# Two-layer hybrid decoder trunk on one core: eight split weight groups in flight at the passage from cross-attention to the up-projection, one token tile first

## What is computed

```python
for l in range(DEPTH):
    y = hybrid_mixer(rms_norm(h, mix_norm_pre[l]), ...)          # attention + convolution heads, one projection out
    h = h + rms_norm(y, mix_norm_post[l])
    y = memory_cross_attention(rms_norm(h, x_norm_pre[l]), rms_norm(mem, mem_norm[l]), wq, wk, wv, wo)
    h = h + rms_norm(y, x_norm_post[l])
    y = conv_ffn(rms_norm(h, ffn_norm_pre[l]), w_up, conv_w, conv_b, w_down)
    h = h + rms_norm(y, ffn_norm_post[l])

def memory_cross_attention(h, mem_n, wq, wk, wv, wo):            # 4 heads of 256, 256 memory tokens
    ...
    return softmax(q k / 16) v @ wo

def conv_ffn(h, w_up, conv_w, conv_b, w_down):                   # w_up: 1024 x 5632, w_down: 2816 x 1024
    u = causal_depthwise_conv(h @ w_up, conv_w, conv_b)          # width 3
    gate, val = u[..., :D_FF], u[..., D_FF:]
    return (gelu(gate) * val) @ w_down
```

## Time and profile before

| | |
|---|---|
| median of 3 runs | 868.9 us (868.72 to 869.17) |
| the profiled execution, its own time | 868.48 us |
| its span, first to last instruction | 866.5 us |
| TensorE busy | 832.1 us (96%) |
| VectorE busy | 616.6 us (71%) |
| ScalarE busy | 498.8 us (58%) |
| mean granted TensorE clock | 0.991 of full speed |

### The profile page before, as it was taken

How to read it: one execution, slowest core, us unless ns; L and a number is a source line. 1 busy time by engine, 2 the same in 40 slices (tenths; PEclk the granted TensorE clock), 3 DMA queues, 4 the chain that set the end, 5 groups by cost and what they waited for, 6 DMA issues and landing times.

```text
span 866.5 us, 13183 instructions
## 1 busy us (share of the span) xinstructions
PE 832.1 (96%) x5252; PEld 742.7 (86%) x5252; DVE 616.6 (71%) x1081; ACT 498.8 (58%) x761; POOL 28.4 (3%) x53
## 2 busy tenths in 40 slices
PE   3999999999979999999999999999998999999997
PEld 2898898888859999988899889887986899999885
DVE  5689986664467877886576999757546587777643
ACT  4655876555447666564454578655645566665441
POOL 1000000010010000000010000001001000000000
PEclk9999999999989999999999999999998999999999
DMA  9555344472344565556646553447433555655651
GB/s 343 206 175 184 105 146 142 150 253 88 121 146 171 196 194 175 178 183 219 193 152 238 168 167 112 139 139 240 149 99 100 166 178 188 196 191 176 206 181 48
DMA packets 40364, 147.33 MB, mean 170 GB/s; under 512 B 4528, under 2 KB 4656, under 8 KB 40304
## 3 DMA queue, kind: packets, MB, share of 16 engines
q1 hardware_dynamic: 38144, 138.90, 49.4%
q0 software_dynamic: 2160, 7.59, 2.6%
HBM read 145.43 MB, written 1.05 MB: 169 GB/s over the span
## 4 chain that ended last, share of the span: by engine, by line
PE 85%; DVE 8%; ACT 2%; issue 2%; DMA 2%; POOL 1%; SPq 0%; DVEq 0%; POOLq 0%; ACTq 0%
PE acc L1303 8%; PE acc L1304 8%; PE acc L1305 8%; PE acc L1279 6%; PE acc L1281 6%; PE acc L1280 6%; DVE wlo L776 3%; PE psAB L1305 3%; PE psAB L1303 3%; PE psAB L1304 3%; PE psAB L1279 2%; PE psAB L1280 2%; PE psAB L1281 2%; PE psCD L1247 2%; PE psCD L1305 2%; PE psCD L1303 2%
## 5 line engine op out<-in xcount | busy, mean ns | idle before, releaser
L776 DVE TENSOR_TENSOR wlo<-raw,whi 128x1024 fp32r<-128x1024 f32 x256 | 307.9, 1221 | 101.4 <-ACT whi L449 98.8
L449 ACT ACTIVATE whi<-raw 128x1024 fp32r<-128x1024 f32 x256 | 267.1, 1057 | 112.2 <-PE acc L1281 51.3
L1303 PE MATMUL acc<-xT_hi,whi 128*128 128x256 f32 x512 | 146.0, 285 | 0.0
L1304 PE MATMUL acc<-xT_lo,whi 128*128 128x256 f32 x512 | 144.8, 283 | 0.0
L1305 PE MATMUL acc<-xT_hi,wlo 128*128 128x256 f32 x512 | 144.8, 283 | 0.0
L1303 PEld LDWEIGHTS acc<-xT_hi,whi 128*128 128x128 f32 x512 | 98.1, 192 | 2.2 <-issue 2.0
L1304 PEld LDWEIGHTS acc<-xT_lo,whi 128*128 128x128 f32 x512 | 98.1, 192 | 0.2
L1305 PEld LDWEIGHTS acc<-xT_hi,wlo 128*128 128x128 f32 x512 | 98.1, 192 | 0.0
L1023 DVE SCALAR_TENSOR_TENSOR arena<-arena,par 128x256 f32<-128x256 f32 x120 | 50.4, 479 | 1.5 <-ACT arena L598 1.5
L1199 DVE SCALAR_TENSOR_TENSOR KT<-acc,par,KT 128x255 f32<-128x255 f32 (+1 forms) x96 | 39.7, 476 | 16.5 <-ACT KT L735 16.1
L1330 PE MATMUL acc<-whi,xT_hi 128*128 128x512 f32 x96 | 40.3, 419 | 6.7 <-DVE xT_lo L883 4.3
(11 more groups left out here) (244 smaller groups left out, 1918.9 us busy)
## 6 DMA issues: line engine op xcount, KB each, us to landing
raw<-stream_dram SPq DMA_DIRECT2D x256, 512.0 KB, 4.1
gpre<-gain_dram POOLq DMA_DIRECT2D x7, 512.0 KB, 5.2
gpost<-gain_dram POOLq DMA_DIRECT2D x6, 512.0 KB, 5.1
memn<-mem_dram SPq DMA_DIRECT2D x2, 512.0 KB, 6.0
h<-x_dram SPq DMA_DIRECT2D x1, 1024.0 KB, 12.2
out_dram<-h SPq DMA_DIRECT2D x2, 512.0 KB, 2.6
cst<-const_dram SPq DMA_DIRECT2D x1, 896.0 KB, 16.6
gpre<-gain_dram SPq DMA_DIRECT2D x1, 512.0 KB, 5.4
```

What stands on the lines that cost most here:

```text
L449: act.activation(whi[:, s * GW:(s + 1) * GW], raw[:, s * GW:(s + 1) * GW], ACT.Copy).then_inc(w_hi.sem, 1)
L776: dve.tensor_tensor(wlo[:, cols], raw[:, cols], whi[:, cols].bitcast(F32), ALU.subtract).then_inc(w_lo.sem, 1)
L1303: pe.matmul(dst, whi[:, cols], hi[:, toks], start=k == 0 and len(outs) == 4, stop=False)
L1304: pe.matmul(dst, whi[:, cols], lo[:, toks], start=False, stop=False)
```

## The change

It alters the passage in both layers, and three things beside it.

- The arena, a region of SBUF that is lent from stage to stage, becomes the first allocation; in it lie four more split weight groups (`held_hi`, `held_lo`). Groups G_XO to G_XO+3 and G_UP to G_UP+3 are split into these, and G_XO+4 to +7 and G_UP+4 to +7 into the ring, so that from G_XO to G_UP+11 a split waits for the group eight before it, not four.
- The product with `wo` takes token tile 0 of all eight groups, then token tile 1 of six of them, then the transposes `inputs(2, 0)`, then token tile 1 of the last two.
- Up tiles 0 and 1 are both made in rows form: token tile 0 of six groups, `inputs(2, 1)`, token tile 0 of two, then token tile 1 of all eight. In the stream the groups of up tile 1 now stand before those of up tile 0 (`load_order`). Both tiles are copied out and transposed (`up_flip`); columns form begins with tile 2.
- `turn(1, ...)` and the steps behind it become `turn_to_up()`, with other places for the splits, and the splits in the loop over j are moved.
- Every columns-form product is packed into two banks, in four pairs for the up-projection (`up_banks`), and the zero matmuls go: the first matmul of each bank has the start flag.
- `gT_hi` and `gT_lo` are interleaved by tile; the down-projection's waits on `y_conv` follow the new banks.

```diff
...
+HELD = 4
+def held(g):
+    return G_XO <= g < G_XO + HELD or G_UP <= g < G_UP + HELD
+def load_order(g):
+    u = g % GROUPS - G_UP
+    return g if not 0 <= u < 2 * HELD else g + (HELD if u < HELD else -HELD)
+def used_before(g):
+    return g + 1 - (RING + HELD if G_XO <= g < G_UP + 2 * HELD + RING else RING)
...
+        held_at = 14 * 1024
+        held_hi = nc.alloc_sbuf_tensor_at("held_hi", [P, HELD * GW], F32R, offset=base + held_at)
+        held_lo = nc.alloc_sbuf_tensor_at("held_lo", [P, HELD * GW], F32R, offset=base + held_at + HELD * GW * 4)
+        assert held_at + 2 * HELD * GW * 4 <= ARENA * 4
...
+        assert taken[0] * 4 <= held_at
+        def home(g):
+            hi, lo = (held_hi, held_lo) if held(g) else (whi, wlo)
+            s = slice(g % RING * GW, (g % RING + 1) * GW)
+            return hi[:, s], lo[:, s]
...
-        up_banks = [[accs[0][0], accs[0][1], accs[1][0], accs[1][1]], psAB + psCD]
+        up_banks = [psAB, accs[1], psCD, accs[0]]
...
-                sp_.dma_start(raw[:, s * GW:(s + 1) * GW], stream[g]).then_inc(raw_in[s].sem, 16)
+                sp_.dma_start(raw[:, s * GW:(s + 1) * GW], stream[load_order(g)]).then_inc(raw_in[s].sem, 16)
             for t in range(TOK):
...
                 act.wait_ge(raw_in[s].sem, raw_in[s].at(l, g // RING + 1))
-                act.wait_ge(w_used.sem, w_used.at(l, g + 1 - RING))
-                act.activation(whi[:, s * GW:(s + 1) * GW], raw[:, s * GW:(s + 1) * GW], ACT.Copy).then_inc(w_hi.sem, 1)
+                act.wait_ge(w_used.sem, w_used.at(l, used_before(g)))
+                act.activation(home(g)[0], raw[:, s * GW:(s + 1) * GW], ACT.Copy).then_inc(w_hi.sem, 1)
...
                     squares_h(l, i + 1, 1)
+                def turn_to_up():
+                    for n in range(2):
+                        act.wait_ge(y_tile0.sem, y_tile0.at(l, 2 + n))
+                        square_y(0, n, n)
+                    split(G_UP)
+                    squares_h(l, 2, 0)
+                    split(G_UP + 3)
+                    act.wait_ge(w_used.sem, w_used.at(l, G_XO + 6))
+                    square_y(1, 0, 0)
+                    input_hi(2, 0)
+                    split(G_UP + 5)
+                    act.wait_ge(w_used.sem, w_used.at(l, G_XO + 2 * PER_TILE))
+                    square_y(1, 1, 1)
+                    split(G_UP + 6)
+                    squares_h(l, 2, 1)
+                    split(G_UP + 7)
+                    input_hi(2, 1)
...
-                split(G_UP + PER_TILE - 1 + AHEAD)
-
-                rows_out(2, G_UP + PER_TILE)
+                turn_to_up()
+                rows_out(1, rows[0], G_UP + HELD)
+                split(G_UP + 2 * HELD + 1)
+                rows_out(0, rows[1], G_UP + 2 * HELD)
+                split(G_UP + 2 * HELD + 3)
...
-                    split(G_UP + (j + 1) * PER_TILE - 1 + AHEAD + (0 if j else 1))
+                    split(G_UP + (j + 1) * PER_TILE - 1 + AHEAD + (2 if j == 1 else 0))
                     gate(j)
...
+                hi, lo = home(g)
+                dve.tensor_tensor(lo, raw[:, cols], hi.bitcast(F32), ALU.subtract).then_inc(w_lo.sem, 1)
...
                     norm_scale(l, i + 1, 1, n_gain)
+                def turn_to_up():
+                    def second(t):
+                        dve.wait_ge(y_sq.sem, y_sq.at(l, 2 * TOK + 2 * t + 2))
+                        dve.scalar_tensor_tensor(st(S_YMS + t), st(S_YSQ + 2 * t + 1), 1.0 / D,
+                                                 st(S_Y0 + t), ALU.mult, ALU.add).then_inc(y_ms.sem, 1)
+                        output_gain(t, 1, 1)
+                    def first(t):
+                        dve.wait_ge(y_sq.sem, y_sq.at(l, 2 * TOK + 2 * t + 1))
+                        first_half(t)
+                        output_gain(t, 0, 0)
+                    first(0)
+                    second(0)
+                    add_output(1, 0)
+                    split(G_UP)
+                    norm_input(l, 2, 0)
+                    norm_scale(l, 2, 0, 2)
+                    split(G_UP + 3)
+                    first(1)
+                    input_lo(2, 0)
+                    split(G_UP + 5)
+                    second(1)
+                    add_output(1, 1)
+                    split(G_UP + 6)
+                    norm_input(l, 2, 1)
+                    norm_scale(l, 2, 1, 2)
+                    split(G_UP + 7)
+                    input_lo(2, 1)
...
+                split(G_UP + 2 * HELD + 3)
                 for j in range(UP_TILES):
-                    split(G_UP + (j + 1) * PER_TILE - 1 + AHEAD + (0 if j else 1))
+                    split(G_UP + (j + 1) * PER_TILE - 1 + AHEAD + (2 if j == 1 else 0))
                     up_taps(j)
...
-                def open_bank(bank):
-
-                    pe.matmul(bank, mT_hi[:, 0:P], zero[:, 0:1].to_broadcast([P, NT]), start=True, stop=False)
-
                 def transposed_product(g0, groups, rhs, outs, k0=0, k_of=KC):
...
                                 pe.matmul(dst, whi[:, cols], lo[:, toks], start=False, stop=False)
                                 e = pe.matmul(dst, wlo[:, cols], hi[:, toks], start=False,
-                                              stop=k == KC - 1 and (c % 2 == 1 or len(outs) == 4))
+                                              stop=k == KC - 1 and c % 2 == 1)
                         e.then_inc(w_used.sem, 1)
...
-
-                def last_product(steps, lhs, k_of, order=None, heads_end=None):
+                def one_tile(g, lhs, dst, k0, t, opens, closes):
+                    hi, lo = lhs
+                    whi_g, wlo_g = home(g)
+                    for u in range(UNITS):
+                        a = slice((k0 + u) * SEQ + t * P, (k0 + u) * SEQ + (t + 1) * P)
+                        cols = slice(u * NT, (u + 1) * NT)
+                        pe.matmul(dst, hi[:, a], whi_g[:, cols], start=opens and u == 0, stop=False)
+                        pe.matmul(dst, hi[:, a], wlo_g[:, cols], start=False, stop=False)
...
+                wo_groups = [(0, 0), (0, 1), (1, 0), (1, 1), (2, 0), (3, 0), (2, 1), (3, 1)]
+                def wo(hd, n, t):
+                    at = wo_groups.index((hd, n))
+                    if not t:
+                        pe.wait_ge(w_lo.sem, w_lo.at(l, G_XO + at + 1))
+                    e = one_tile(G_XO + at, O, acc[n][t], 2 * hd, t, hd == 0, hd == X_HEADS - 1)
+                    if t:
+                        e.then_inc(w_used.sem, 1)
+                    elif hd == X_HEADS - 1:
+                        e.then_inc(y_tile0.sem, 1)
                 pe.wait_ge(xo_lo.sem, xo_lo.at(l, 1))
-                wo(0, 0)
+                wo(0, 0, 0)
                 x_values(1)
                 x_flip(2)
-                wo(0, 1)
+                wo(0, 1, 0)
                 pe.wait_ge(xo_lo.sem, xo_lo.at(l, 2))
-                wo(1, 0)
+                wo(1, 0, 0)
                 x_values(2)
                 x_flip(3)
-                wo(1, 1)
+                wo(1, 1, 0)
                 pe.wait_ge(xo_lo.sem, xo_lo.at(l, 3))
                 x_values(3)
-                g = G_XO + PER_TILE
-                last_product([(g, 4, 0, False), (g + 2, 4, 1, False), (g + 1, 6, 0, True), (g + 3, 6, 1, True)], O, KC,
-                             heads_end=KC)
+                wo(2, 0, 0)
+                wo(2, 1, 0)
+                pe.wait_ge(xo_lo.sem, xo_lo.at(l, X_HEADS))
+                wo(3, 0, 0)
+                wo(3, 1, 0)
+                for hd, n in wo_groups[:6]:
+                    wo(hd, n, 1)
                 inputs(2, 0)
-
-
-                for j in range(UP_TILES):
-                    if j >= 2:
-                        pe.wait_ge(y_conv.sem, y_conv.at(l, j - 1))
-                    if j == 0:
-                        first_product(2, G_UP, X, acc[0])
-                    elif j == 1:
-                        transposed_product(G_UP + PER_TILE, 1, X, up_banks[1])
-                        for t in range(TOK):
-                            pe.wait_ge(rows_in.sem, rows_in.at(l, TOK + t + 1))
-                            for c in range(4):
-                                e = pe.transpose(up_chunk(0, c)[:, t * P:(t + 1) * P],
-                                                 rows[:, t * NT + c * P:t * NT + (c + 1) * P], ident)
-                        e.then_inc(u_tr.sem, 1)
-                        transposed_product(G_UP + PER_TILE + 1, 3, X, up_banks[1], k0=2)
-                    else:
-                        transposed_product(G_UP + j * PER_TILE, PER_TILE, X, up_banks[j % 2])
-                G = (gT_hi, gT_lo)
-                pe.wait_ge(y_conv.sem, y_conv.at(l, UP_TILES - 1))
+                for hd, n in wo_groups[6:]:
+                    wo(hd, n, 1)
+                def up(i, t):
+                    g = G_UP + i
+                    if not t:
+                        pe.wait_ge(w_lo.sem, w_lo.at(l, g + 1))
+                    k0 = i % HELD * UNITS
+                    if k0 % 4 == 0:
```

(74 more changed lines are left out.)

56 lines of the change are left out of this document (24 added, 32 removed).

## The result

The changed kernel takes 859.9 us (median of 4 runs, 859.2 to 861.6) against 868.85 us before: ratio 0.9898, 95% interval 0.9883 to 0.9914. It is 1.0% faster; 862.1 us was forecast.

A forecast was written before the change was run, and what follows sets the result against it. TensorE, busy 96% of the span, was taken to bound the kernel. From the profiled 868.5 us, - 16.4 - 3.9 + 13.6 gives 861.8; adding 0.4 for the median gives 862.1 us, range 857 to 866.5.

The forecast's parts named there:

- term one: Passage from `wo` to up tile 2: 53.6 us against 61.8 per layer, clock staying up; -16.4 us in all.
- E: Time mark in each layer: the end of the last rows-form matmul, from which later steps are counted in us.
- No slack: Token tile 1's line to the second `xn` transposes: 0.1 us of standing, each further us late costing one us.
- rival of late rows: Token tile 1's rows late at `inputs(2, 1)`, TensorE standing 2 us per layer: 866 to 868, 8%; slower than before, 5%.
- term two: Twenty zero matmuls removed, ten openings of two: nine at 0.43 us each count, -3.9 us.
- nine are behind a busy TensorE: Of ten zero-matmul openings, all but the first at the start save their 0.43 us.
- term three: New stall behind the passage, at group G_UP+13, with the clock's fall: 6.8 us in each layer, +13.6 us.
- TensorE stands 4.7 us: Wait in both layers for the split of G_UP+13, queued behind two tiles of gating; the clock adds 2.1 us.
- Interleaving `gT`, the arena's place, ... cost nothing: These, the stream's order and `y_conv` were said to cost nothing: same instructions, same shapes, banks reused later.
- No stall: Rival: no wait at G_UP+13 because gating overlaps more than thought; 848.6 us, chance 6%.
- The stall without the fall of the clock: Rival: TensorE waits at G_UP+13, but the gap is too short for the clock to fall; 858.4 us, chance 10%.

The follow-up runs named there:

- e1: Changed kernel with only the places of the weight splits moved in the loop over j, on ScalarE and VectorE: 846.6 us, ratio 0.974.
- e2: Kernel before without the twenty zero matmuls, the first matmul of each bank having the start flag: 866.5 us, ratio 0.9967.
- e8: Kernel of e1 with two idle 128x1024 subtractions on VectorE ahead of norm_input(2, 1): 854.5 us, ratio 0.9821 to the kernel before.
- e9: Changed kernel with eighteen idle 128x512 matmuls on TensorE between groups G_UP+12 and G_UP+13: 856.4 us, ratio 0.9854 to the kernel before.
- e5: Kernel before with the arena and `gT` as first SBUF allocation, ahead of `raw` (byte 16512), start rounded to 32 bytes: 866.4 us, ratio 0.9967.
- e6: Kernel before with the arena and `gT` moved ahead of `memn` (about byte 131200): 865.85 us, ratio 0.9964.
- e3: Kernel before with `gT` starting 32 bytes later, at a multiple of 64 bytes: 869.0 us, ratio 0.9997.
- e4: Kernel before with `gT` interleaved by tile at the old place: 868.9 us, ratio 0.9999.
- e7: Changed kernel with the split ahead of gate(1) reaching G_UP+13, not G_UP+12, on both engines: 858.2 us, ratio 0.988 to the kernel before.

## Why the prediction was right, point by point

**The passage, term one (-16.4).** It held, a little short. E lies 51.96 us behind the first `wo` matmul for 51.9 by my sum; no wait is left there, and the clock stays up. Of the whole term e1 gives a check, since it has no stall: its stretch takes 157.8 us in each layer where the kernel before takes 165.6 and 165.7, 15.7 less in all for 16.4. The rest of the 22.0 us between their spans is 3.4 in the down-projections and 2.9, which is what e2 gives for the zero matmuls. "No slack" at the second `xn` transposes was too strict by 0.5 us (e8), and the rival of late rows was real in its mechanism, at 3.9 us per layer for 2.5 of delay. ScalarE did wait for one load in this line, 0.57 us; the sum had 0.7 there.

**The zero matmuls, term two (-3.9).** Mis-sized: e2 gives 2.9. The step that failed is "nine are behind a busy TensorE": TensorE was busy at all nine, but behind two of them, one in each layer, it meets VectorE within one group, and busy time doesn't show a wait that is just met.

**The stall, term three (+13.6).** It held: 13.7 by the stretches of e1 and the changed kernel, 13.3 by their medians. The step "TensorE stands 4.7 us" measured 4.6, the split of G_UP+13 ended when I said (E+20.7 for E+20.8), and e1 shows that its place in the two lists was the whole cause. The clock's share, 2.1, measured 2.2 by the starts behind the wait, 2.1 in e1 and 1.9 to 2.0 in e9. There is luck in that. The low stretch had 5.05 us of work in it where I took 4.1 to 5.1 and went by the lower end; but work at the lower level doesn't lose half, as I wrote, since a 128x256 costs 0.213 us there and 0.12 at the full clock. The two errors cancel. My reading of the earlier trace rows was a little off as well: they put the low stretch of the kernel before at 243.79 to 250.62 us, 6.8 long, not at 243.85 to 250.55.

**The step that was wrong**: "Interleaving `gT`, the arena's place, ... cost nothing: the same instructions on the same shapes". The same instructions took 389 ns in place of 396, and 3.4 us of the span's 7.8 come from there, by the arena's place alone (e5, e6).

**The sum.** The result lies 2.2 us below the forecast. Of this, 1.1 lies between the executions and not in the mechanism: I added 0.4 to get from the profiled execution to the median, and the changed kernel's profiled execution lay 0.7 above its median instead. Between the profiled executions 1.1 is left: the arena's place took 3.4 off, the removed openings and the later start gave 1.5 less than the 3.9 forecast, and the passage with its stall 0.8 less than the 2.8. So the errors cancel in large part, and the total is nearer than its terms.

**The rivals.** *No stall* is ruled out, for it was there. *The stall without the fall of the clock* is ruled out too: the clock fell in both layers of the profiled execution, and the others' mean clocks, 0.991 to 0.993, show falls as well. *Late rows* didn't happen, but e8 shows their price, larger than I gave. So of some 19 us that the passage and the zero matmuls give, 13.7 were given back, some 16 us behind E in each layer, by a list of splits that wasn't moved along.

## What to carry to other kernels

Where a change makes two tiles finish together that came one after the other, write down for every in-order engine what now stands in a row behind them, and put the next feeds of the bound engine into the idle times between its steps: here the same work in another order was worth 13 us of 860. A wait of TensorE costs itself and often the slow clock behind it, so it pays to remove it whole, not to move it by one group. And a busy engine hides waits that are just met: each removed instruction is worth its time only up to the next of them.

## What the runs showed of the hardware

- The place of a tensor in SBUF changed the time of the matmuls that have it as stationary operand: 396 ns (0.233 us from start to start) with `gT` from 179872 to 224928 of a partition, 389 ns (0.227) at 16512 (after, e5) and at 131200 (e6), whatever its alignment to 64 bytes (e3) or interleaving (e4). Where between the two the border lies, and why, wasn't tried.
- A wait of 2.0 us with the transposes of `xn` behind it was enough for the clock to fall (e8, both layers of the profiled execution); it then stayed low for 3.4 us. It doesn't always fall: one of e8's five executions kept a mean of 0.999, and in layer two of e7 a wait of 2.67 us left the clock up where one of 1.94 us, 5 us later, didn't. In e7 it stayed low for 3.4 us too, and behind the 4.6 us of the changed kernel for 6.8.
- The lower clock costs less than twice the time: a 128x256 takes 0.213 us from start to start in place of 0.12 (after), a 128x512 0.43 in place of 0.23 (e8).
- Eighteen idle matmuls in each of the two waits took 3.9 us off the two stretches, 3.5 off the median (e9). The Trainium skill ("TensorE: Matmul & The Clock Gate", section "Why this matters for your kernels") asks that TensorE be kept from idle gaps between bursts; here work that nobody needs did it, and the trace agrees: the granted clock stays at 1.00 behind the filled wait.
